# A hybrid diffusion block on one core: two product groups move from the last half steps of the state-space scan to the place after its last rotation

## The reference, cut to what matters

```python
h = RMSNorm(x) * (1 + scale1) + shift1
P = h @ W_in            # columns go to: GLA, S5, Hyena, three gates
y_hy  = hyena_mix(...)  # short convolution of P's 1536 Hyena columns, then two FFT long convolutions
y_gla = GLA(...)        # gated linear attention, both directions
y_s5  = S5(...)         # complex diagonal state space, both directions, then GELU and GLU
mix = W_out( sum_b sigmoid(g_b) * (y_b @ W_b) );  x += gate1 * mix
x += gate2 * SwiGLU(RMSNorm(x) * (1 + scale2) + shift2);  output RMSNorm(x) * g_final
```

## Time and profile before

| | |
|---|---|
| median of 3 runs | 1220.31 us (1219.78 to 1221.37) |
| profiled execution | 1222.88 us, its span 1221.1 us |
| PE busy | 1112.5 us, 91% |
| DVE, ACT, POOL busy | 589.4, 401.3, 335.2 us |
| mean granted TensorE clock | 0.946 of full |

### The profile page before, as it was taken

The page is one execution under the profiler, slowest core; times in us unless marked ns, Lnnn a source line. Parts: engine busy times, 40 slices in busy tenths (PEclk is TensorE's granted clock), DMA queues, the critical chain, the costliest instruction groups (busy, mean ns, idle before and its releaser), DMA issues.

```text
span 1221.1 us, 15749 instructions
## 1 busy us (share of the span) xinstructions
PE 1112.5 (91%) x6109; PEld 847.9 (69%) x6109; DVE 589.4 (48%) x1135; ACT 401.3 (33%) x763; POOL 335.2 (27%) x288
## 2 busy tenths in 40 slices
PE   4799989978989999998997979798999999999995
PEld 1368948866667676777473654697888888888884
DVE  3775156576598888883196966445000012000013
ACT  2762323443344544432411100234323212232221
POOL 2032212501300000000131210352655545665540
PEclk9899989988989998998998989898999999999998
DMA  9820223765222223313323237561333233333211
GB/s 316 270 103 27 70 69 130 130 150 174 69 61 87 88 70 71 86 58 101 144 86 120 69 109 260 178 183 48 104 104 92 73 94 104 104 104 104 78 44 70
DMA packets 139367, 134.32 MB, mean 110 GB/s; under 512 B 12937, under 2 KB 125865, under 8 KB 138268
## 3 DMA queue, kind: packets, MB, share of 16 engines
q1 hardware_dynamic: 126448, 105.52, 29.5%
q0 software_dynamic: 3744, 16.15, 3.6%
q10 hardware_dynamic: 9100, 11.64, 3.2%
HBM read 120.18 MB, written 11.01 MB: 107 GB/s over the span
## 4 chain that ended last, share of the span: by engine, by line
PE 56%; DVE 13%; issue 3%; ACT 2%; DMA 1%; ACTq 1%; POOL 0%; DVEq 0%; POOLq 0%
PE psum L746 49%; PE psum L1006 1%; PE psum L1109 1%; PE psum L986 1%; DMA buf<-in_w_out 1%; PE psum L779 1%; DVE ring_lo L2056 1%; PE psum L999 1%; DVE buf L2132 1%; ACTq L1582 1%; DVE hT_lo L2395 1%; PE psum L974 1%; DVE buf L2102 1%; DVE buf L2309 1%; DVE buf L2105 1%
## 5 line engine op out<-in xcount | busy, mean ns | idle before, releaser
L1298 POOL TENSOR_TENSOR ring_lo<-buf,ring_hi 128x512 fp32r<-128x512 f32 (+2 forms) x220 | 282.1, 1314 | 504.9 <-ACT ring_hi L1453 504.9
L746 PE MATMUL psum<-hT_hi,ring_hi 128*128 128x512 f32 x712 | 286.8, 403 | 8.7 <-DVE hT_lo L2395 4.0
L746 PE MATMUL psum<-hT_lo,ring_hi 128*128 128x512 f32 x712 | 280.2, 394 | 0.0
L746 PE MATMUL psum<-hT_hi,ring_lo 128*128 128x512 f32 x712 | 279.9, 393 | 0.0
L1453 ACT ACTIVATE ring_hi<-buf 128x512 fp32r<-128x512 f32 (+1 forms) x260 | 139.6, 610 | 227.7 <-PE psum L746 161.6
L746 PE MATMUL psum<-buf,buf 128*128 128x512 f32 (+1 forms) x368 | 152.2, 570 | 21.9 <-issue 15.4
L746 PEld LDWEIGHTS psum<-hT_hi,ring_hi 128*128 128x128 f32 x712 | 135.7, 191 | 42.6 <-issue 5.4
L746 PEld LDWEIGHTS psum<-hT_lo,ring_hi 128*128 128x128 f32 x712 | 135.9, 191 | 28.7 <-issue 1.7
L746 PEld LDWEIGHTS psum<-hT_hi,ring_lo 128*128 128x128 f32 x712 | 135.4, 190 | 29.1
L746 PEld LDWEIGHTS psum<-buf,buf 128*128 128x128 f32 x368 | 68.9, 207 | 94.3 <-issue 85.4
L2404 DVE TENSOR_TENSOR buf<-psum,buf 128x512 f32<-128x512 f32 x22 | 15.2, 692 | 221.5 <-PE psum L746 221.5
(11 more groups left out here) (333 smaller groups left out, 1694.0 us busy)
## 6 DMA issues: line engine op xcount, KB each, us to landing
buf<-in_w_in SPq DMA_DIRECT2D x26, 1024.0 KB, 5.1
buf<-in_w_mod SPq DMA_DIRECT2D x24, 1024.0 KB, 8.2
buf<-in_w_ffn_in SPq DMA_DIRECT2D x44, 512.0 KB, 5.1
buf<-in_w_ffn_out SPq DMA_DIRECT2D x8, 1024.0 KB, 5.0
scr_k<-buf POOLq DMA_DIRECT2D x4, 1024.0 KB, 5.5
buf<-scr_k POOLq DMA_DIRECT2D x4, 1024.0 KB, 7.9
buf<-in_w_out SPq DMA_DIRECT2D x4, 1024.0 KB, 6.6
buf<-in_w_ffn_out SPq DMA_DIRECT2D x4, 768.0 KB, 4.6
```

What stands on the lines that cost most here:

```text
L746: ins = nc.tensor.matmul(o, a, b, start=start and n == 0, stop=stop and n == len(pairs) - 1)
L1298: nc.gpsimd.tensor_tensor(ring_lo[:, a:a + n], ring[:, a:a + n], ring_hi[:, h + i * n:h + i * n + n].bitcast(fp32), SUB)\
```

## The change

```diff
@@ -552,13 +552,13 @@
                 step("s5_y", b - 1)
             if m + 2 < 2 * NB:
                 step("s5_v", *divmod(m + 2, 2))
-            one_beside(m % 3 != 2)
+            one_beside(m % 3 != 2 and m < 12)
             if m + 2 < 2 * NB:
                 step("s5_w", *divmod(m + 2, 2))
                 step("s5_k", *divmod(m + 2, 2))
-        step("s5_y", NB - 1)
         while late or beside:
             one_beside()
+        step("s5_y", NB - 1)
```

## The result

| | before | changed |
|---|---|---|
| median of 20 runs | 1218.85 us (1216.0 to 1221.68) | 1223.97 us (1220.31 to 1227.99) |
| ratio | | 1.0044, 95% interval 1.0034 to 1.0054 |
| profiled execution's span | 1221.1 us | 1223.8 us |
| PE busy | 1112.5 us | 1109.1 us |
| mean granted TensorE clock | 0.946 | 0.951 |

The kernel is 5.1 us slower, while PE is busy for less time and at a higher clock: the time went into waits. (The median of 20 runs of before lies 1.5 us under the one of 3 that the prediction had.)

A forecast was written before the change was run, and what follows sets the result against it. PE is busy 91% of the span, so its waits and clock count. +3.6 us up to `hy_tok` and +1.6 after `s5_y(7)` make 5.2, said as +5.0: 1225.3 us, forecast's own range 1222.8 to 1227.8, overall 1220.8 to 1229.2.

The forecast's parts named there:

- Half step 12: PE waits some 2.0 us for `V9` ahead of `s5_k` of half step 14; `hy(3,1)` then takes 7.2 us.
- Half step 13: DVE runs 2.65 us sooner, `V9` of half step 15 done at 534.15 us; `s5_k` then takes 1.01 us.
- Half step 14: After PE's waits, `hy(4,0)` runs at half clock, 7.19 us, then `s5_d` 0.81 and `s5_y(6)` 3.25 us.
- The new wait: Half step 15: 7.96 us from `s5_y(6)` to L2056's end, covered only by `hy(4,1)`; PE waits 2.4 us ahead of `hy(5,0)`.
- POOL beside L2056: POOL's low half of `gate20` overlaps DVE's L2056 and lengthens it by 0.4 us, bounds 0 and 0.6.
- Half clock in `hy(5,0)`: The clock falls after the 2.8 us wait ahead of `hy(5,0)`, which takes 7.19 us: 1.6 us more.
- From there: From `hy(5,0)` through `hy(5,1)` and `s5_y(7)`: `hy_tok` starts at 570.8 us instead of 567.2, +3.6 us.
- The tail: After `s5_y(7)`, PE waits around 4 us for the stores and `merge_g` starts at half clock: +1.6 us.
- The load of `gate02`: In SP's queue it now comes just before the stores and may hold them up: 0 to 1 us, taken as 0.
- The rival of the clock: The clock stays up after the waits: no change, 1220.3 us, or up to 1222.7 with one or two falls; 20%.
- The longer half clock: Half clock lasts twice as long at three places, 1.6 us each, plus 1 us for `gate02`: up to +9.9 us; 15%.
- the rival that ended faster: PE runs from `s5_k` to `hy_tok` without a stop, the chain under 5.58 us: -2.4 us, 1217.9 us; 7%.

The follow-up runs named there:

- e8: Changed kernel, but only half step 12 gives its second group away, so one group is left over and not two; 1210.56 us, ratio 0.9943 to before.
- e2: Changed kernel with DVE's low half of `hy5` two steps sooner, ahead of the evacuation of `hy(4,0)`; 1219.88 us, ratio 1.0008 to before.
- e5: Changed kernel with the low half of `gate20` on DVE again and POOL doing nothing there; 1224.04 us, ratio 1.0041 to before.
- g1: Changed kernel with `merge_g(2,0,0)` ahead of `hy_tok` and the GELU's reload issued as soon as the stores landed; 1223.78 us, ratio 1.0038 to before.
- e3: Changed kernel, but only half step 13 gives its second group away, so one group is left over and not two; 1217.64 us, ratio 0.9989 to before.
- f2: Kernel before, with half step 12 giving its second group away and half step 14 taking one; 1212.88 us, ratio 0.9958 to before.
- e4: Changed kernel with `merge_g(2,0,0)` and its sigmoid ahead of `hy_tok`; 1231.04 us, ratio 1.0108 to before.
- e7: Kernel before with `merge_g(2,0,0)` ahead of `hy_tok`; 1225.51 us, ratio 1.0065 to before.
- e6: Changed kernel with only half step 13 giving a group away and `merge_g(2,0,0)` ahead of `hy_tok`; 1224.43 us, ratio 1.0053 to before.
- e1: Changed kernel with `s5_y(7)` ahead of `hy(5,0)` and `hy(5,1)`, as in the kernel before; 1227.06 us, ratio 1.0071 to before.

## Why the prediction was right

The sign, the place and the size were right: +5.0 us forecast, +5.1 measured (ratio 1.0044, interval 1.0034 to 1.0054). How close the two came is luck, since the terms below sum to some 4.3 us in the profiled execution. Point by point, in before's time:

- *Half step 12.* A wait of 2.0 us ahead of `s5_k`: 1.97. e8 has the same wait and is fast, so it is hidden behind DVE, as costed. `hy(3,1)` took 6.28 us and not 7.2, hidden too.
- *Half step 13.* `V9` of half step 15 2.65 us sooner: 2.57 (533.33 - 513.67 against 536.80 - 514.57). Right. But `s5_k` took 1.83 us at half clock, not 1.01.
- *Half step 14.* `hy(4,0)` 7.19 us: 7.74. Half clock was granted over 6.2 us, `s5_k` taken in. With the 0.8 us of `s5_k` above, the forecast was too small here by 1.4 us.
- *The new wait.* The chain from `s5_y(6)` to the end of L2056 7.96 us: 554.97 - 547.02 = 7.95. Wait 2.4 without POOL's part: 2.36. Right, and e2, which moves that low half alone, has no such wait and gains 2.3 us in the distance.
- *POOL beside L2056.* 0.4 us: none (2.36 us as before). The contention came one instruction later, where nobody waited (e5).
- *Half clock in `hy(5,0)`*, 1.6 us: none. A wrong step, of nearly the same size as what `s5_k` and `hy(4,0)` took more.
- *From there.* +3.6 us at `hy_tok`: +3.0.
- *The tail.* A wait of some 4 us: 3.16; half clock in `merge_g` 1.6 us: 12.60 - 11.15 = 1.45 us from `merge_g` to `glu`. Right in the profiled execution. g1 shows that it isn't a term one can take out by filling the wait. The load of `gate02` held no store up: from the start of `hy_tok` to the first L1635 it took 6.6 us (569.32 to 575.92) and 6.8 us before (567.20 to 573.97).
- *The rival of the clock.* The forecast counted three falls behind `s5_k`; two came. "One or two of them" is what that rival allows, so as to the clock it was the one that came true, and only its price was off: it added two falls up to 2.4 us, while two at its own 1.6 are 3.2, and the two measured 0.8 in `s5_k`, 2.2 in `hy(4,0)` (7.74 against 5.58) and 1.45 in `merge_g`, 4.4 us together. (The longer half clock is mis-added too: 5.0 + 3 times 1.6 + 1 is 10.8 and not 9.9 us.)

So two clock terms were off in opposite directions, by 1.4 and 1.6 us, and the total was luckier than its parts. The mechanism (PE's work behind `s5_k` exceeds what DVE's earlier finish gives, and a low half late by 2.4 us) was shown by e2, e3 and e8; the rival that ended faster fell with the chain, which took 7.95 us and not under 5.58. What isn't shown by an experiment is the price of half clock in `merge_g`: it is read from the rows, and no run takes it away without moving it. The nearest is the pair of e8 and f2, with one order on PE and the clock up or down in `merge_g`: 1.4 us there, 1.3 in the distance.

What the prediction didn't see is that giving away one group from half step 12 gains what giving away two loses. In the changed kernel DVE's gain of 2.6 us at `V9` is paid with four groups behind `s5_k` that had been two; e8 has the same early `V9` (527.73 + 0.76 - 508.83 = 19.66 us behind `s5_y(5)`, the same 19.66 as the changed kernel) with three, and the fourth fills PE while it would wait for DVE.

## What to carry to other kernels

Filler work is worth most where the other engine sets the pace: before moving it, find for each place which engine the two meet behind, and move one unit at a time, since the second can cost what the first gained. When an order is changed, follow each helper step that is placed by counting (here a low half six steps behind its split): it moves too, and it can land behind a chain that nobody waited for. An idle wait that is filled only pays if what stands behind it, here a reload in a busy queue, doesn't become the later one.

## What the runs showed of the hardware

- GpSimd beside VectorE. L2161, with two inputs in SBUF, took 1.51 us beside POOL's L1298 and 0.42 us alone, 3.6 times as long; L2201, with an input in PSUM, took 0.75 us beside it (at 559.38 us) and alone. The Trainium skill (GPSIMD Engine Reference, Key points) names VectorE's instructions with two SBUF inputs among those that contend with GpSimd; these rows agree in kind. But L2056, with two such inputs, kept its 2.36 us over the 0.9 us that it shared with POOL's first instruction. That instruction took 2.06 us and the next three 1.47 each, of the 6.37 us in this row, so there it may have been POOL that paid; no run here separates the two.

```profile
554.13 6.37 POOL L1298 TENSOR_TENSOR ring_lo<-buf,ring_hi 128x512 fp32r<-128x512 f32 x4 [231.70 <-ACT ring_hi L1453]
```

- TensorE's clock. It stayed at full behind waits of 2.36 us (between product groups, changed kernel) and 3.08 us (behind `hy_tok`, e8), and was at the lower level behind 1.88 us and 2.31 us beside short matmuls, and soon after 3.16 us (changed kernel) and 3.26 us (f2) at the place where e8 had 3.08. So the length of a wait alone didn't decide it in these runs.
- The reload of 1 MB took 7.3 us when issued ahead of POOL's four loads; issued behind them it took 12.4, 9.5, 7.6 and 7.1 us at 0.4, 2.2, 4.1 and 7.8 us behind the last of them (e4, e7, e6, e1).
